# Two heads' products in turns in a state-space scan on TensorE, with plain VectorE forms and an earlier attention order

## The reference, cut to what matters

```python
cb = jnp.einsum('bclgn,bcsgn->bcgls', cm, bm)
y_diag = jnp.einsum('bcgls,bcgrls,bcsgrp->bclgrp', cb, decay, xdt)
...
y_off = jnp.einsum('bclgn,bcgrpn,bclgr->bclgrp', cm, prev, jnp.exp(a_cs))
y = y_diag + y_off + d_skip.astype(jnp.float32).reshape(g_, r_)[:, :, None] * xs
```

```python
p = jax.nn.softmax(logits, axis=-1)
outs.append(jnp.einsum('bhqk,bkhd->bqhd', p, vf[:, :q1]))
```

## Time and profile before

| what | value |
|---|---|
| median of 3 runs | 2647.3 us (2646.77 to 2648.64) |
| time of the profiled execution | 2652.36 us |
| span in the trace, first to last instruction | 2650.2 us |
| mean granted TensorE clock, as a share of full speed | 0.963 |
| scan's head loops of groups 0, 1, 2, 3, about | 108 to 175, 209 to 291, 326 to 407, 439 to 491 us |
| attention's steps, about | 1904 to 2078 us |

### The profile page before, as it was taken

One profiled execution on the slowest core, in us unless ns is written; L12 is line 12 of the kernel. 1 busy time (PEld: TensorE's weight loads), 2 busy tenths in 40 slices (PEclk: granted clock), 3 DMA queues, 4 the chain that ended last, 5 costly groups with the idle time before them and its releaser, 6 DMA issues.

```text
span 2650.2 us, 31446 instructions
## 1 busy us (share of the span) xinstructions
PE 2455.3 (93%) x12039; PEld 1971.2 (74%) x12039; DVE 881.1 (33%) x1430; ACT 892.7 (34%) x1243; POOL 1208.9 (46%) x1012
## 2 busy tenths in 40 slices
PE   6999998889999998888888999999899989999997
PEld 5676776658888766667676888877678778979886
DVE  3344453332112221555543211222444222323232
ACT  2332323252333343443435233334422124323222
POOL 3455454434444436655653444444411234645552
PEclk8899998989999999999998999999999999999999
DMA  4212222113222212111112322222211111332321
GB/s 120 64 48 64 64 64 64 32 63 103 91 91 95 95 53 89 41 47 47 42 62 65 103 95 84 90 95 62 77 48 33 49 48 48 96 96 81 95 87 56
DMA packets 230834, 188.87 MB, mean 71 GB/s; under 512 B 8831, under 2 KB 222268, under 8 KB 230604
## 3 DMA queue, kind: packets, MB, share of 16 engines
q1 hardware_dynamic: 227024, 183.66, 22.6%
q10 hardware_dynamic: 3708, 3.79, 0.5%
HBM read 185.30 MB, written 2.10 MB: 71 GB/s over the span
## 4 chain that ended last, share of the span: by engine, by line
PE 85%; POOL 5%; issue 4%; ACT 3%; DVE 2%; DMA 0%; SPq 0%; ACTq 0%; DVEq 0%; POOLq 0%
PE ps L2338 51%; PE ps L2430 11%; PE ps L1249 7%; PE ps L613 2%; POOL w_lo L1648 2%; PE ps L2547 1%; PE ps L2369 1%; PE ps L2528 1%; PE ps L1219 1%; PE ps L2550 1%; PE ps L1357 1%; PE ps L1308 1%; PE ps L2465 1%; PE ps L1353 1%; POOL hdd L396 1%
## 5 line engine op out<-in xcount | busy, mean ns | idle before, releaser
L1648 POOL TENSOR_TENSOR w_lo<-raw,w_hi 128x512 fp32r<-128x512 f32 (+2 forms) x712 | 903.0, 1300 | 1019.2 <-ACT w_hi L1796 1019.1
L2338 PE MATMUL ps<-a_hi,w_hi 128*128 128x512 f32 (+1 forms) x1424 | 505.8, 375 | 43.1 <-POOL a_lo L1664 20.3
L1796 ACT ACTIVATE w_hi<-raw 128x2048 fp32r<-128x2048 f32 (+2 forms) x178 | 327.7, 1841 | 550.1 <-PE ps L2338 381.3
L2338 PE MATMUL ps<-a_hi,w_lo 128*128 128x512 f32 (+1 forms) x1424 | 500.9, 372 | 0.5 <-issue 0.5
L2338 PE MATMUL ps<-a_lo,w_hi 128*128 128x512 f32 (+1 forms) x1424 | 500.3, 372 | 0.0
L2338 PEld LDWEIGHTS ps<-a_hi,w_hi 128*128 128x128 f32 x1424 | 261.3, 191 | 106.3 <-issue 46.7
L2338 PE MATMUL ps<-b_hi,w_hi 128*128 128x512 f32 x784 | 309.0, 394 | 3.2 <-DVE hv L1193 3.0
L2338 PE MATMUL ps<-b_hi,w_lo 128*128 128x512 f32 x784 | 310.1, 396 | 0.0
L2338 PE MATMUL ps<-b_lo,w_hi 128*128 128x512 f32 x784 | 308.3, 393 | 0.0
L2338 PEld LDWEIGHTS ps<-a_hi,w_lo 128*128 128x128 f32 x1424 | 261.2, 192 | 47.8 <-issue 1.0
L2338 PEld LDWEIGHTS ps<-a_lo,w_hi 128*128 128x128 f32 x1424 | 260.3, 191 | 48.2
(11 more groups left out here) (313 smaller groups left out, 3430.8 us busy)
## 6 DMA issues: line engine op xcount, KB each, us to landing
raw<-in_mlp_w_dram SPq DMA_DIRECT2D x128, 512.0 KB, 4.2
raw<-in_w_up_dram SPq DMA_DIRECT2D x44, 512.0 KB, 4.9
raw<-in_ssd_w_in_dram SPq DMA_DIRECT2D x40, 512.0 KB, 4.8
raw<-in_hgrn_w_in_dram SPq DMA_DIRECT2D x24, 512.0 KB, 4.5
raw<-in_w_in_dram SPq DMA_DIRECT2D x24, 512.0 KB, 5.2
raw<-in_ssd_w_out_dram SPq DMA_DIRECT2D x16, 512.0 KB, 4.3
raw<-in_ple_w_gate_dram SPq DMA_DIRECT2D x16, 512.0 KB, 4.5
raw<-in_w_down_dram SPq DMA_DIRECT2D x16, 512.0 KB, 4.4
```

Source lines behind the costliest of these rows:

```text
L1648: last = nc.gpsimd.tensor_tensor(w_lo[:, slot, piece], raw[:, slot, piece], w_hi[:, slot, piece].bitcast(F32), ALU.subtract)
L1796: nc.scalar.activation(w_hi[:, slot, 0:n], raw[:, slot, 0:n], ACT.Copy).then_inc(whi_ready, 1)
L2338: last = nc.tensor.matmul(ps[:, b + s, 0:nn], w[:, k, m * P:(m + 1) * P], v[:, k, c0 + s * nn:c0 + (s + 1) * nn], start=(k == 0 and first) ...
```

## The change

On PE the loop over heads becomes a loop over pairs. Both heads' pours come first, then the waits for both heads, then the 14 products, alternating between the two heads (so between the two halves of the array's columns). `bcast` of a head moves with them. On DVE `decay(g, r + 2)` goes behind `y_tile` and `ssd_evict`; on ACT `exp_cs` of odd heads goes behind `ssd_cuts`. In the attention `values(n)` moves from between two parts of the fill to behind `turn_p(n + 1)`. On DVE ten places go from `scalar_tensor_tensor` to `tensor_tensor` (eight) or `tensor_scalar` (two: the attention's `normed`, L1068, and the first tap of the last feed-forward part's convolution, L1181).

```diff
@@ tensor, group(g)
-                for r in range(HPG):
-                    if r + 2 < HPG:
-                        bcast(r + 2)
-                    pour("b", g, r)
-                    j, q0 = r // 2, 64 * (r % 2)
+                for j in range(HPG // 2):
+                    heads = (2 * j, 2 * j + 1)
+                    if j:
+                        bcast(2 * j + 1)
+                    pour("b", g, 2 * j)
+                    if 2 * j + 2 < HPG:
+                        bcast(2 * j + 2)
+                    pour("b", g, 2 * j + 1)
                     yb = bank[6 + j % 2]
...
-                    pe.wait_ge(m_ready, g * 8 + (r + 1))
-                    pe.wait_ge(ch_ready, g * 8 + (r + 1))
+                    pe.wait_ge(m_ready, g * 8 + (2 * j + 2))
+                    pe.wait_ge(ch_ready, g * 8 + (2 * j + 2))
                     for c in range(NCH):
                         cols = slice(c * P, (c + 1) * P)
-                        last = nc.tensor.matmul(yb[q0:q0 + 64, cols], xdt[:, c, r * 64:(r + 1) * 64],
-                                                em[r % 3][:, cols], start=True, stop=(c == 0))
+                        last = [nc.tensor.matmul(yb[64 * (r % 2):64 * (r % 2) + 64, cols], xdt[:, c, r * 64:(r + 1) * 64],
+                                                 em[r % 3][:, cols], start=True, stop=(c == 0)) for r in heads]
                         if c:
-                            last = nc.tensor.matmul(yb[q0:q0 + 64, cols], hst[:, c - 1, r * 64:(r + 1) * 64],
-                                                    eh[r % 3][:, cols], start=False, stop=True)
+                            last = [nc.tensor.matmul(yb[64 * (r % 2):64 * (r % 2) + 64, cols],
+                                                     hst[:, c - 1, r * 64:(r + 1) * 64],
+                                                     eh[r % 3][:, cols], start=False, stop=True) for r in heads]
@@ vector, after mult
-                    if r + 2 < HPG:
-                        decay(g, r + 2)
                     if r % 2 == 0 and r:
                         y_tile(g, r // 2 - 1)
                     ssd_evict("b", g, r, keep=("c", 5))
+                    if r + 2 < HPG:
+                        decay(g, r + 2)
@@ tensor, attention
-                half = per_step[s] // 2 if n < N_FOX - 2 else 1
-                if qb:
-                    fill(half)
-                    values(n)
-                    fill((per_step[s] if n < N_FOX - 2 else 3) - half)
-                else:
-                    fill(per_step[s] if n < N_FOX - 2 else 3)
+                fill(per_step[s] if n < N_FOX - 2 else 3)
                 if n + 1 < N_FOX:
                     turn_p(n + 1)
+                if qb:
+                    values(n)
@@ vector, one of the eight to tensor_tensor, and the two to tensor_scalar
-                        nc.vector.scalar_tensor_tensor(out=b_lo[:, k, 0:T], in0=hv[:, k % 4], scalar=1.0,
-                                                       in1=b_hi[:, k, 0:T].bitcast(F32), op0=ALU.mult,
-                                                       op1=ALU.subtract).then_inc(blo_ready, 1)
+                        nc.vector.tensor_tensor(b_lo[:, k, 0:T], hv[:, k % 4], b_hi[:, k, 0:T].bitcast(F32),
+                                                ALU.subtract).then_inc(blo_ready, 1)
...
-                nc.vector.scalar_tensor_tensor(out=fp[0:q, n % 2, 0:nk], in0=fp[0:q, n % 2, 0:nk],
-                                               scalar=fm[0:q, n % 2, 3:4], in1=ones[0:q, 0:1].broadcast_to([q, nk]),
-                                               op0=ALU.mult, op1=ALU.mult).then_inc(f_pn, 1)
+                nc.vector.tensor_scalar(fp[0:q, n % 2, 0:nk], fp[0:q, n % 2, 0:nk], fm[0:q, n % 2, 3:4], None,
+                                        ALU.mult).then_inc(f_pn, 1)
...
-                    own.did(nc.vector.scalar_tensor_tensor(out=acc[:], in0=au[:, 4:516], scalar=taps[2],
-                                                           in1=taps[3].broadcast_to([P, T]), op0=ALU.mult, op1=ALU.add))
+                    own.did(nc.vector.tensor_scalar(acc[:], au[:, 4:516], taps[2], taps[3], ALU.mult, ALU.add))
```

More of the change, by code:

```diff
@@ L1082, in roped @@
                     dve.wait_ge(r_sin, 2 * i + (e + 1))
-                    nc.vector.scalar_tensor_tensor(out=t, in0=t, scalar=1.0, in1=fv[e][:], op0=ALU.mult,
-                                                   op1=ALU.add).then_inc(r_rope, 1)
+                    nc.vector.tensor_tensor(t, t, fv[e][:], ALU.add).then_inc(r_rope, 1)
             def decayed(i, e, kb):
@@ L2061, in summed @@
                         own.wait()
[L2062 to L2063 removed]
+                    ins = nc.vector.tensor_tensor(lv[:, 0:T], res[:, 0, 0:T] if m == 1 else lv[:, 0:T], res[:, m, 0:T],
+                                                  ALU.add)
                     if m < KD - 1:
```

40 lines of the change are left out of this document (19 added, 21 removed).

## The result

| what | before | changed |
|---|---|---|
| median of the first comparison | 2647.97 us (4 runs) | 2603.18 us (4 runs) |
| median of the second comparison | 2646.22 us (9 runs) | 2604.23 us (5 runs) |
| time and span of the profiled execution | 2652.36, 2650.2 us | 2603.32, 2601.2 us |
| mean granted clock | 0.963 | 0.970 |

The ratio is 0.9826, 95% interval 0.9807 to 0.9845, in the first comparison and 0.9844 (0.9831 to 0.9858) in the second: 42 to 45 us faster. The direction and the likeliest case, overlap, came true; the forecast had the medians 32 us apart, so the gain is 10 to 12 us larger than forecast.

A forecast was written before the change was run, and what follows sets the result against it. TensorE, busy 93% of the span, was taken to bound the kernel nearly everywhere. Terms summed to 32.8 us off 2652.4, 2619.6 profiled; less 5.1 for the median, 2615 us, range 2604 to 2642.

The forecast's parts named there:

- the likeliest case, overlap: Scan products on TensorE: neighbours in different halves of the array's columns stream together; 2615 us, chance 0.50.
- change of width and products in turns: Scan's head pairs: 2.4 us from 16 fewer runs of 64-column products, 19 us from both halves streaming together.
- first pair's wait: TensorE's wait on GpSimd's `decayed_c` in groups 0, 2 and 3, covered by two pours: 3.0 + 1.8 + 1.2 us less.
- clock behind it: TensorE's lower clock after that wait: 4 us won in group 0, 1 in group 3.
- longer chain in group 3: Group 3's later pairs wait for the second head's chain off TensorE: 0.9 + 0.1 + 0.6 us more.
- attention and forms in it: Attention's new order 1 us less (2 less to 4 more saved); VectorE forms, two `tensor_scalar`, another 1 us.
- Some loads will not hide, so of the 24.4 I take 19: Pair's 28 weight loads in 1.53 us, 55 ns each: just fits, so the gain is set at 19 us.
- the bound of 24.4: Most that turns could gain in the scan if 14 products take the time of seven: 16 x 1.53 us.
- The rival of a changeover at each turn: Switching halves costs TensorE up to 0.15 us at each of 224 products: 2667 us, slower; chance 0.09.
- 3.8 to 5.2 us stay: Group 3's first-pair wait: two slices cover only part of 5.6 + 0.97 us, saving 0.4 to 1.8 us.
- the `bcast` run before it: Group 0's clock fall: another possible reason than the 2.97 us wait; then its 4.8 us might not return.
- `values` waits for ScalarE's copy, 2.1 us in four pieces: Attention: this TensorE wait goes with the whole fill and a turn between; net 1 us less taken.

The follow-up runs named there:

- scan alone: The kernel before with only the scan's pairs on TensorE and the VectorE and ScalarE orders that go with them: 2615.2 us, 0.9874 of before.
- turns of a chunk: The changed kernel with a pair's products alternating chunk by chunk (`em` and `eh` product of one head, then the other's): 2601.4 us, 0.9818 of before.
- three `bcast`: The changed kernel with `bcast(2)` put back ahead of each group's first pour, so three stand in a row: 2602.4 us, 0.9837 of before.
- w_lo chunk behind: The changed kernel with GpSimd's `decayed_c` of heads 0 and 1 ahead of the group's first `w_lo` chunk: 2595.3 us, 0.9804 of before.

## Why the forecast was right in kind and short in size

The terms for the profiled pair, 2652.4 to 2603.3 us. Group 2 has no fall in either kernel, so its 8.2 us less the 1.8 of its wait give what pairs and turns are worth in a group, 6.4 us. In the other groups the remainder is taken as the clock's (group 0: 14.3 less 6.4 and 2.0 of wait; group 1: 7.9 less 6.4; group 3: 4.6 less 6.4, and its waits of 0.8 and 0.9 us more added back):

| term | forecast | measured |
|---|---|---|
| change of width and products in turns | 21.4 | 25.6 |
| first pair's wait | 6.0 | 3.0 (2.0, 1.8, and 0.8 longer in group 3) |
| clock behind it | 5 (0 to 10) | 7.3 (5.9, 1.5, 0, 0) |
| longer chain in group 3 | 1.6 more | 0.9 more |
| attention and forms in it | 2 | 12.1 |
| rest (1.5 of it the fall at 317.3 us, ahead of group 2) | 0 | 1.9 |
| sum | 32.8 | 49.0 |

*The turns.* The mechanism was right: two streams run side by side in the two halves, and 28 loads of 64 columns fit into the time of 14. The step that failed is "Some loads will not hide, so of the 24.4 I take 19": all hide. In its products a pair saves a whole head's 1.68 us, that is 16 x 1.68 = 26.9 us, the bound of 24.4 and the 2.4 of the joints together. The loops keep 1.6 us of it a pair, 25.6 in all: the new order puts three `bcast` of a group between two pours, and each starts 0.32 us behind the pour's last record, where 0.23 is usual. The Trainium skill ("TensorEngine Tiling (Array Packing)", Key Properties) says that tiles operate independently; this trace agrees, two streams at one record in 0.109 us each. The Trainium skill ("TensorE: Matmul & The Clock Gate", Part 3) lets weight loads overlap with running products only where the row groups differ. All rows are in use here in both halves, and 14 products with their 28 loads of 146 ns in 1.68 us contradict it. The rival of a changeover at each turn is excluded: the 14 products with 13 turns take no longer than seven.

*The first pair's wait.* For groups 0 and 2 it was nearly right (3.0 and 1.8 us forecast, 2.0 and 1.8 measured); the 0.9 us left in group 0 is there because the fall of 3.4 us, which had held TensorE back ahead of its wait, is gone. Group 3 failed in sign: "3.8 to 5.2 us stay" was 6.5. Its clock no longer fell during the two pours, so TensorE came to the wait 6.2 us behind `bcast(0)`, as before with half the slices (6.1 us), while what it waits for came 1 us later. Wait and clock have to be priced together here: where a chain off TensorE sets the end, faster work ahead of it only makes the wait longer. Groups 1 and 2 of before show the same: one had a fall and no wait, the other a wait of 1.82 us and no fall, and the loops differ by 0.3 us.

*The clock.* Its bounds held, and that "the `bcast` run before it" might be the reason was named; the runs show falls behind such a run and behind a wait, and neither alone explains them all. What was missed is that one profiled execution's falls are a draw: 13.6 us at the lower clock in group 0 there, 3.4 us in two other executions of the same loop. The pair of profiles overstates the gain (49.0 against 42 to 45 us by medians). The 5.1 us that I took off for the median belonged to this one long execution of before; the changed kernel's profiled execution lies at its median (2603.3 against 2603.2 us). So the profiled time was missed by 16 us and the median only by 12, and the smaller miss is luck.

*The longer chain.* Forecast 0.9, 0.1 and 0.6 us of wait in the three pairs, measured none, 0.3 and 0.6. The first has none because it runs at the lower clock, where two pours and two `bcast` last 9.7 us. In the four other kernels in which the clock was back up by then, or had not fallen, and which keep this order (scan alone, turns of a chunk, three `bcast`, w_lo chunk behind) it waits 0.76 us for VectorE's `mult`, as this chain was added up.

*The attention* is where the forecast missed its range. The step that failed: "`values` waits for ScalarE's copy, 2.1 us in four pieces", with "TensorE is busy for 167.8 of the 174 us, so there is not more to win". There were 12 us to win. First, I counted of the 6.2 us of idle only the pieces that named the line that moves, and not the 3.2 us on VectorE's eviction, which the move also sets earlier. Second, busy time is no bound: a record of 0.27 us that is usually followed at 0.11 us hides up to 0.16 us of the gap behind it, and the joints between widths are hidden in the same way. So a step that shrank by 0.72 us (5.09 to 4.37) shows only 0.36 us of idle before, and those that shrank by 0.1 us show none. Third, two falls of the clock of 3.4 us each lay in this stretch, worth some 3 us, and are gone; without them the order gives 9 us. I asked what the turn would wait for in the new place, and not what waits for the fill's last slice, which moved ahead.

*The forms.* Right: nothing alone, to within some 4 us. In the trace `tensor_scalar` is shorter than what it replaced, the shape of 400 columns 428 against 635 ns, and the swap to `tensor_tensor` of `b_lo` (L2106 before) left the median of one at 693 ns, as the earlier trace rows had it:

```profile
L1067 DVE TENSOR_SCALAR fp<-fp,fm 128x400 f32<-128x400 f32 x8 | 3.4, 428 | 0.3
```

The Trainium skill ("VectorE: DVE Perf Modes", The perf-mode tier table) gives fp32 `tensor_scalar` in SBUF twice the rate of `tensor_tensor`. The trace agrees for the part that grows with the columns: from 144 to 528 columns the usual duration rises from 296 to 495 ns, where with `scalar_tensor_tensor` it rose from 370 to 770 ns. TensorE gained at most 0.3 us by it in the attention's steps.

Of the 16.2 us that the sum missed in the profiled pair, 10.1 are the attention's, 4.2 the turns', 2.3 the clock's, 1.9 the rest's and 0.7 the shorter chain's, and 3.0 went the other way with the wait. With the attention right the forecast would have been 2605 us, inside its range and 1 to 2 us from the medians.

## What to carry to other kernels

Products that fill half of the array's columns cost next to nothing when they run beside another stream in the other half (14 here in the 1.68 us of seven): issue them in turns of one or two products, and count the joints that the new order makes elsewhere. Price a move by what waits for each instruction that changes place, also on other engines' queues, and not by the waits that name it; TensorE's busy time is no bound on what is lost, distances between starts are. Compare loops of several executions before giving a price to the clock. Where a chain off TensorE sets the end, shorten that chain first, as the 9 us of one reordered chunk show.

## What the hardware showed that was not expected

- TensorE ran four records ahead into the other half when both heads came one after the other (2.82 us for 14 products, neither 1.68 nor 3.36), and not further.
- Two streams of fp32 products with 64-column weights kept exactly the pace of one, 0.109 us a record, with loads of 146 ns each, so that a load goes in every 0.055 us.
- At full clock a 512-column record of the pours follows the last at 0.232 us (the median), at the lower level at 0.427: a microsecond there costs 0.46, not 0.5.
- A product of another width costs time where it meets a dense stream: `bcast` and the 64-column products start 0.32 us behind the last record of a pour in place of 0.23.
- The clock fell within 4.2 us in 8 of 12 loops that open with three products of 8 rows in a row (3.2 us), TensorE being busy throughout, and in none of 27 that open with two. It also fell behind a wait of 1.15 us among thin products. The same loop showed 3.4 or 13.6 us of it in different executions.
